# One first norm over seven tiles: the memory's tokens ahead of the rows, with the memory's key and value projection woven in

## The chip, the cores and the metric

The kernel runs on one core of a Trainium2 chip. The metric is the device time of one execution in microseconds. Engines are named as in the profile: PE is TensorE (PEld its weight loads), DVE is VectorE, ACT is ScalarE, POOL is GpSimd, SP is SyncE, which here issues nearly all DMAs. All data is float32. A large product is made in three matmuls on float32r operands: each operand is split into a high part (ACT casts it) and a low part (DVE or POOL subtracts the high part from the original), and high x high, low x high and high x low are summed in PSUM.

## The reference

Two transformer blocks run one after the other. The parts that the change touches, shortened:

```python
h = concatenate([meta, x])                       # 16 + 512 tokens, 1024 wide
u = rmsnorm(h, mix_norm_g);  proj = u @ w_in     # block 1: token mixer, then
h = h + token_mixer(u)                           # an expert-choice FFN with
h = h + expert_choice_ffn(rmsnorm(h, ffn_norm_g))#   16 experts
...
mkv = rms_norm(mem, mem_norm_w) @ w_mem_kv       # block 2: mem is 256 x 1024,
mk, mv = split(mkv)                              #   w_mem_kv 1024 x 1536
mqn = rms_norm(mq, mem_q_norm_w); mk = rms_norm(mk, mem_k_norm_w)
y_mem = softmax(mqn @ mk.T * 192**-0.5) @ mv     # 4 heads of 192
merged = g0*(y_ssd @ w_ssd_br) + g1*(y_dil @ w_dil_br) + g2*(y_mem @ w_mem_br)
h = h + merged @ w_out
h = h + peer(rms_norm(h, norm_ffn_w))            # 16384 experts, top 16 x 8
```

`mem` is an input: its norm and its product with `w_mem_kv` depend on nothing that either block computes.

## The kernel before, in words

The program is a sequence of blocks (`nc.Block()`); in each, every engine has its own list of instructions, and all engines meet at the block's end. Beside the block's own work runs a **feed** (class `Feed`): a list of weight chunks (1024 x 256 columns, 1 MB) and of jobs on them. A job is one PSUM result (128 tokens x 256, or 128 channels x 264 or 512), made in 24 matmuls when k is 8. The feed is cut into **ticks**, one job each, and every block is allotted some ticks; each engine's list holds its part of a tick at a place written out by hand:

- SP (L602): loads the next chunk into one of two raw slots, after the low part of the chunk in that slot was taken (`low_done`); also stores results that go to DRAM.
- ACT (L691): casts a chunk's high part, after the last job on the chunk two before it (`product_done`).
- POOL (L711): subtracts to get the low part. For the very first chunk DVE does it (`first_low`, L702).
- PE (L630 to L652): job n, after the result of job n - `banks` was taken out of PSUM (`taken`). `banks` is 2 in block 1's mixer (`proj_mix`) and 3 in block 2's merge (`proj_br`).
- `take_out`: in tick t the engine named by a job (ACT or DVE) takes out the job of tick t - (banks - 1), in its program order.

`normalise` (L134 to L330) does a norm with transposition: for tile n of 128 rows ACT squares and sums (L179), DVE forms 1/(mean + eps), ACT takes the root (L214) and scales (L187), PE transposes in 8 matmuls (L317), DVE multiplies by the gain (L254), ACT takes the high part two tiles later (`take_high`, L193) and DVE the low part (`take_low`, L258). In block 1's first norm (`norm1`, five tiles: four of x and the 16 meta tokens) the feed has one tick, in which the first chunk is split; the jobs begin in the next block.

In block 2 the merge (L3590 to L3660) runs these blocks, each with ticks of `proj_br`: `load_mem` (mem and two gains; 3 ticks), `norm_mem` (the memory's norm; 5), `turn_ssd` (4), `norm_mq` (`rms_groups` over the four query tiles; 6), `turn_mq` (2), a bare `run_to` (2, and x comes back from DRAM), `norm_mk` (2), `turn_mk` (1), and `attend` (L2464), the attention to the memory in 18 rounds, with 3 ticks, at rounds 5, 11 and 17. The jobs are 8 for the dilated branch (k = 2, DVE takes them out), 12 for the memory's keys and values (`mkv_jobs`, ACT takes them out into `mkv`), 8 for the SSD branch (DVE: a product with the gate and a sum), then 8 for the memory branch and 16 for `w_out`.

`norm2`, ahead of the experts' routing, loads `gain_row` at its own beginning (L293), and DVE waits for it before anything else.

Of the kernel before, what the change touches and what calls it, by code (L numbers as in the profile page):

```python
# [23 lines left out]
P = 128  # L24
# [109 lines left out]
def normalise(nc, name, x, tiles, gain_col, ident, xT, gain_row=None, kept=None, feed=None, prime=False, loads=(), late_loads=(),  # L134
              ahead=None, tile_product=None, tile_loads=None, side_loads=()):

    n_tiles = len(tiles)
    split = isinstance(xT, tuple)  # L140
    with Stage(nc, name) as st:
# [12 lines left out]

        def turned_of(n):
            return turned[:, n % 2, :].rearrange("p (k c) -> p k c", k=KD)[:, :, 0:tiles[n][1]]
# [4 lines left out]
        def part(buf, n):  # L161
            _, rows, col = tiles[n]
            return buf[:, :, col:col + rows]

# [4 lines left out]
        with nc.Block() as block:  # L169

            @block.scalar
            def _(act):
                def square(n):
# [5 lines left out]
                    act.activation(squares[:rows, :] if kept is None else kept[:rows, i, :], x[:rows, i, :],  # L179
                                   ACT.Square, accum_out=ssq[:rows, n:n + 1]).then_inc(squared, 1)  # L180

                def scale_here(n):
# [4 lines left out]
                    act.activation(row(n), x[:rows, i, :], ACT.Copy, scale=rstd[:rows, n:n + 1]  # L187
                                   ).then_inc(scale_done, 1)

                def take_high(n):  # L190
                    if kept is None:
                        act.wait_ge(gain_done, n + 1)
                        act.copy(part(xT[0], n), to_split(n)).then_inc(high_done, 1)  # L193
                    elif split:
                        act.wait_ge(turn_done, n + 1)
                        act.copy(part(xT[0], n), to_split(n)).then_inc(high_done, 1)
                    else:
                        act.wait_ge(turn_done, n + 1)
                        act.copy(part(xT, n), turned_of(n)).then_inc(evac_done, 1)
                    if feed is not None and not prime:  # L200
                        feed.act(act, n + 1, n_tiles + 1)
# [5 lines left out]
                for n in range(n_tiles):  # L207
# [11 lines left out]
                    if prime and n == n_tiles - 2:  # L219
                        feed.act(act)  # L220
                for n in range(max(0, n_tiles - 2), n_tiles):
                    take_high(n)

            @block.vector
            def _(dve):
                order = InOrder(dve, dve_order)
                dve.memset(ssq[:, :], 1.0).then_inc(cleared, 1)
                if loads:
                    dve.wait_ge(loaded, 16 * len(loads))
                if feed is not None:  # L230
                    feed.dve(dve, 0, n_tiles + 1)
# [8 lines left out]
                def scale(n):  # L240
                    i, rows, _ = tiles[n]
                    dve.wait_ge(rooted, n + 2)
# [3 lines left out]
                def apply_gain(n):  # L246
# [6 lines left out]
                    gain = gain_col.unsqueeze(2).broadcast_to([P, KD, rows])  # L253
                    dve.tensor_tensor(to_split(n), turned_of(n), gain, ALU.mult).then_inc(gain_done, 1)  # L254

                def take_low(n):
                    dve.wait_ge(high_done, n + 1)
                    dve.tensor_tensor(part(xT[1], n), to_split(n), part(xT[0], n).bitcast(F32),  # L258
                                      ALU.subtract).then_inc(evac_done, 1)
                    if feed is not None:  # L260
                        feed.dve(dve, n + 1, n_tiles + 1)

                behind = 2 if kept is not None else 1 if feed is None or prime else 0
                invert(0)
                for n in range(n_tiles):
# [8 lines left out]
                if prime:  # L274
# [3496 lines left out]
```

## Time and profile before

| what | us |
|---|---|
| median of 3 runs | 4327.09 (4322.07 to 4329.12) |
| the profiled execution | 4337.45 |
| its span | 4335.6 |
| PE busy | 4023.7 (93%) |
| DVE busy | 3022.6 (70%) |
| ACT busy | 2296.2 (53%) |
| POOL busy | 1200.4 (28%) |
| granted TensorE clock, mean | 0.961 of full |
| first block (norm1) | 0 to 27.1 |
| norm2 | 487.5 to 507.5 |
| merge, `load_mem` to the end of `attend` | 2719.5 to 2919.5 |

The profiled execution took 1.85 us more than its span, and 10.4 us more than the median of the runs. A busy share of PE is not its share of peak: a matmul at half clock, and one whose end is modelled, counts as busy as well. [...]

### The profile page before, as it was taken

How to read it: one execution, taken by the hardware profiler on the slowest of the kernel's cores; microseconds unless marked ns; L12 is line 12 of the kernel's file. 1: busy time of each engine (PE TensorE's matmuls, PEld its weight loads, DVE VectorE, ACT ScalarE, POOL GpSimd, SP SyncE). 2: the span in 40 equal slices, each digit the busy share in tenths (PEclk: the TensorE clock that was granted, in tenths of full speed). 3: DMA queues.
4: the chain of work that ended last, by engine and by line, in shares of the span. 5: the costliest groups of instructions: out<-in, count | busy, mean ns of one | idle time of the engine just before them, and what ended most of it. 6: DMA issues, size and time to landing. Idle time of an engine off the chain costs nothing. (4 is left out here: it accounts for less than half of the span.)

```text
span 4335.6 us, 58000 instructions
## 1 busy us (share of the span) xinstructions
PE 4023.7 (93%) x21773; PEld 3180.7 (73%) x21773; DVE 3022.6 (70%) x3734; ACT 2296.2 (53%) x2943; POOL 1200.4 (28%) x555
## 2 busy tenths in 40 slices
PE   8888599999999999999699899788999999999999
PEld 7776566666666666666589777667889999978887
DVE  4365478888888888888445532443599777788885
ACT  4432266777776767776344345322237988333332
POOL 2210201000000100000222221312254555666762
PEclk9999799999999999999899899788999999999999
DMA  3211479999999999998323331413256999999995
GB/s 101 90 63 61 154 306 370 368 372 373 370 363 369 380 368 374 374 378 326 129 90 114 136 99 40 141 58 99 84 194 212 327 349 346 364 350 368 367 368 190
DMA packets 294884, 1082.18 MB, mean 250 GB/s; under 512 B 23234, under 2 KB 163778, under 8 KB 246568
## 3 DMA queue, kind: packets, MB, share of 16 engines
q1 hardware_dynamic: 254136, 936.49, 57.9%
q0 software_dynamic: 40560, 143.16, 8.9%
q8 instruction: 121, 1.98, 0.2%
q14 instruction: 67, 0.55, 0.0%
HBM read 1001.57 MB, written 77.97 MB: 249 GB/s over the span
## 5 line engine op out<-in xcount | busy, mean ns | idle before, releaser
L1789 ACT CAST moe_expert_high<-moe_expert_raw 128x2048 fp32r<-128x2048 f32 x570 | 973.4, 1759 | 383.2 <-DMA moe_expert_raw<-in_w_down_blocks 121.2
L1558 DVE TENSOR_TENSOR moe_expert_low<-moe_expert_raw,moe_expert_high 128x2048 fp32r<-128x2048 f32 x380 | 817.5, 2197 | 170.7 <-ACT moe_expert_high L1789 170.2
L3124 ACT CAST peer_high<-peerbuf_table_raw 128x1024 fp32r<-128x1024 f32 x256 | 256.0, 1049 | 432.9 <-PE peer_ps L3107 281.0
L711 POOL TENSOR_TENSOR branches_proj_low<-branches_proj_raw,branches_proj_high 128x2048 fp32r<-128x2048 f32 (+3 forms) x58 | 246.5, 4250 | 683.7 <-ACT branches_proj_high L691 627.8
L1676 POOL DMA_INDIRECT scratch_h<-ffn_result,ffn_y_rows x16 | 65.2, 4074 | 1223.0 <-DVE ffn_result L1828 1223.0
L1558 DVE TENSOR_TENSOR ffn_expert_low<-moe_expert_raw,moe_expert_high 128x2048 fp32r<-128x2048 f32 (+1 forms) x192 | 362.6, 1929 | 52.2 <-ACT moe_expert_high L1789 52.1
L3078 PE MATMUL peer_ps<-peerbuf_hnT_high,peer_high 128*128 128x384 f32 x1024 | 352.6, 344 | 5.2 <-ACT peer_high L3124 5.2
L3079 PE MATMUL peer_ps<-peerbuf_hnT_low,peer_high 128*128 128x384 f32 x1024 | 345.1, 337 | 0.0
L2927 DVE TENSOR_TENSOR peer_low<-peerbuf_table_raw,peer_high 128x1024 fp32r<-128x1024 f32 x185 | 255.7, 1410 | 123.4 <-ACT peer_high L3124 121.9
L1718 PE MATMUL ffn_gate_p<-moe_expert_high,ffn_x_high 128*66 128x512 f32 (+1 forms) x768 | 284.1, 376 | 1.2 <-DVE ffn_x_low L1858 1.2
L1719 PE MATMUL ffn_gate_p<-moe_expert_high,ffn_x_low 128*66 128x512 f32 (+1 forms) x768 | 283.1, 375 | 0.0
L1718 PE MATMUL ffn_up_p<-moe_expert_high,ffn_x_high 128*66 128x512 f32 (+1 forms) x768 | 282.5, 374 | 0.0
L1719 PE MATMUL ffn_up_p<-moe_expert_high,ffn_x_low 128*66 128x512 f32 (+1 forms) x768 | 282.3, 374 | 0.0
L1745 PE MATMUL ffn_down_p<-moe_expert_high,ffn_t_high 128*66 128x512 f32 x704 | 280.0, 398 | 0.3 <-ACT moe_expert_high L1789 0.3
L1747 PE MATMUL ffn_down_p<-moe_expert_high,ffn_t_low 128*66 128x512 f32 x704 | 277.2, 394 | 0.0
L2927 POOL TENSOR_TENSOR peer_low<-peerbuf_table_raw,peer_high 128x1024 fp32r<-128x1024 f32 x71 | 185.7, 2620 | 231.4 <-ACT peer_high L3124 231.4
L3107 PE MATMUL peer_ps<-peer_high,peerbuf_hnT_high 128*128 128x512 f32 x768 | 238.6, 392 | 9.9 <-DVE peerbuf_hnT_low L3194 6.1
L3107 PE MATMUL peer_ps<-peer_low,peerbuf_hnT_high 128*128 128x512 f32 x768 | 237.4, 390 | 0.0
L3107 PE MATMUL peer_ps<-peer_high,peerbuf_hnT_low 128*128 128x512 f32 x768 | 237.4, 390 | 0.0
L3088 PE MATMUL peer_ps<-peerbuf_hnT_high,peer_low 128*128 128x384 f32 x1024 | 202.1, 339 | 6.8 <-DVE peer_low L2927 5.9
L3078 PEld LDWEIGHTS peer_ps<-peerbuf_hnT_high,peer_high 128*128 128x128 f32 x1024 | 194.6, 190 | 5.4 <-ACT peer_high L3124 5.4
L711 POOL TENSOR_TENSOR mix_proj_mix_low<-mix_proj_mix_raw,mix_proj_mix_high 128x2048 fp32r<-128x2048 f32 (+2 forms) x24 | 90.0, 3749 | 386.0 <-ACT mix_proj_mix_high L691 386.0
(552 smaller groups left out, 9425.3 us busy)
## 6 DMA issues: line engine op xcount, KB each, us to landing
moe_expert_raw<-in_w_gate_blocks SPq DMA_DIRECT2D x80, 2048.0 KB, 9.2
moe_expert_raw<-in_w_up_blocks SPq DMA_DIRECT2D x80, 2048.0 KB, 9.5
moe_expert_raw<-in_w_down_blocks SPq DMA_DIRECT2D x80, 2048.0 KB, 9.9
peerbuf_table_raw<-in_peer_down_t SPq DMA_DIRECT2D x64, 1024.0 KB
peerbuf_table_raw<-in_peer_up_t SPq DMA_DIRECT2D x64, 1024.0 KB
branches_proj_raw<-in_w_in SPq DMA_DIRECT2D x36, 1024.0 KB, 5.3
scratch_a<-peer_gelu SPq DMA_DIRECT2D x64, 384.0 KB
scratch_g<-peer_spread SPq DMA_DIRECT2D x24, 1024.0 KB
```

The lines of the kernel that those rows point to most:

```text
L711: pool.tensor_tensor(owner.slot_of(owner.low, at), owner.slot_of(owner.raw, at), owner.slot_of(owner.high, at).bitcast(F32), ALU.subtract) ...
L1558: return engine.tensor_tensor(self.half_of(self.low, q, h), self.half_of(self.raw, q, h), self.half_of(self.high, q, h).bitcast(F32), ALU. ...
L1718: pe.matmul(out, x_high[:, k, 0:CAP], hi[:, k, :], start=(k == 0), stop=False)
L1719: pe.matmul(out, x_low[:, k, 0:CAP], hi[:, k, :], start=False, stop=False)
L1745: pe.matmul(down_p[:CAP, cols], t_high[:, s, t, 0:CAP], hi[:, t, cols], start=(c == 0 and t == 0), stop=False)
L1747: pe.matmul(down_p[:CAP, cols], t_low[:, s, t, 0:CAP], hi[:, t, cols], start=False, stop=False)
L1789: act.copy(half_of(high, q, h), half_of(raw, q, h)).then_inc(high_done, 1)
L2927: return engine.tensor_tensor(low[:, q % 2, cols], raw[:, q % PR_RAW, cols], high[:, q % 2, cols].bitcast(F32), ALU.subtract)
L3078: pe.matmul(out_t, d_high[:, j, k, :], hn_high[:, k, 0:DTOK], start=(k == 0), stop=False)
L3079: pe.matmul(out_t, d_high[:, j, k, :], hn_low[:, k, 0:DTOK], start=False, stop=False)
L3107: last = pe.matmul(ps[:, 2 * t + half, :], lhs, right[:, q % 2, cols], start=(b == 0 and j == 0 and c == 0 and right is high), stop=(b == ...
L3124: act.copy(high[:, q % 2, cols], raw[:, q % PR_RAW, cols]).then_inc(high_done, 1)
```

## The change

- `normalise` can take a `head`: tiles of another buffer, with a gain and a result of their own, that pass ahead of its tiles; and a list `beside` that puts feed ticks behind each tile on ACT, DVE and PE. `norm1` now passes seven tiles: two of `mem`, four of x, the meta tokens. The 12 key and value jobs are the first of `proj_mix`; DVE takes them into staging, and SP stores them to a new DRAM buffer `mkv_dram`. `beside=[[], [0], [], [1, 2, 3], [4, 5, 6], [7, 8], [9, 10], [11, 12]]`.
- In SP's list the loads are mem 0, mem 1, identity, two column tables, x 0, x 1, then tick 0 of the feed, then x 2, x 3, the meta tokens, then the other ticks.
- In the merge `norm_mem`, the 12 jobs, the bare `run_to` and `norm_mk` are gone. `load_mem` loads `mkv` from DRAM. `turn_ssd` has 3 ticks. `norm_mq` and `norm_mk` are one `rms_groups` over six tiles (`norm_mqk`, 7 ticks), and x comes back there. `turn_mq` has 1 tick, `turn_mk` 1, `attend` 1, at round 17.
- `gain_row` of `norm2` is loaded during the last stretch of the mixer; DVE waits for it only before it scales the first tile. The router's weights are issued ahead of the feed's part.

The core of the diff:

```diff
@@ normalise, ACT
+                    ticks_at(feed.act if beside else None, act, n)
                 for n in range(max(0, n_tiles - 2), n_tiles):
                     take_high(n)
+                ticks_at(feed.act if beside else None, act, n_tiles)
@@ normalise, DVE
                         apply_gain(n)
+                    if beside and n == 1:
+                        feed.first_low(dve)
                     if split and n >= behind:
                         take_low(n - behind)
+                    ticks_at(feed.dve if beside else None, dve, n)
...
+                ticks_at(feed.dve if beside else None, dve, n_tiles)
@@ normalise, SP
                         for to, at in side_loads:
                             sp.dma_start(to, at).then_inc(side_in, 16)
+                    if n == 3 and beside:
+                        feed.sp(sp, 0, beside[-1][-1] + 1)
@@ normalise, PE
                     last.then_inc(turn_done, 1)
+                    if beside and beside[n] and n == n_mem + 1:
+                        pe.wait_ge(evac_done, n_mem)
+                    ticks_at(feed.pe if beside else None, pe, n)
@@ first_block
+            def memory(n):
+                return [Job("token", 0, 256, lambda nc, ps, slot: nc.vector.tensor_copy(slot, ps), "dve", col=col, rows=rows,
+                            store=mkv_dram[i, :, n * 256:(n + 1) * 256]) for i, rows, col in mem_tiles]
...
+                      head=(mem, cols_2[:, a:a + n], mem_uT, N_MEM // P),
+                      beside=[[], [0], [], [1, 2, 3], [4, 5, 6], [7, 8], [9, 10], [11, 12]])
...
-                          loads=[(gain_row[:, :], io["ffn_g_row"].partition_broadcast(P))],
+                          gain_in=gain_in,
@@ second_block
-                feed.allot_to(dil_end)
-                normalise(nc, "norm_mem", mem, mem_tiles, gain("mem_g"), ident, mem_uT, feed=feed)
-                feed.allot(4)
+                feed.load("load_mem", [(mkv[:, i, :], mkv_dram[i]) for i in range(N_MEM // P)] +
...
+                feed.allot(3)
                 turn_rows(nc, "turn_ssd", y_ssd, SEQ_TILES, ident, ssdS, feed=feed)
-                feed.allot(6)
-                rms_groups(nc, "norm_mq", [mq[:, i, :] for i in range(NT)], HEADS, MEM_HD, q_gain[:, :], feed)
+                feed.allot(7)
+                rms_groups(nc, "norm_mqk", [mq[:, i, :] for i in range(NT)] + [mkv[:, i, 0:MEM_W] for i in range(N_MEM // P)],
+                           HEADS, MEM_HD, [q_gain[:, :]] * NT + [k_gain[:, :]] * (N_MEM // P), feed,
+                           [(x[:, 0:NT, :], x_dram, x_back)])
-                feed.allot(2)
+                feed.allot(1)
                 turn_rows(nc, "turn_mq", mq, SEQ_TILES, ident, mqT, MEM_W // P, feed)
-                feed.run_to(mkv_end + feed.lag, lambda sp: sp.dma_start(x[:, 0:NT, :], x_dram).then_inc(x_back, 16))
-                mem_side.stack.close()
-                feed.allot(2)
-                rms_groups(nc, "norm_mk", [mkv[:, i, 0:MEM_W] for i in range(N_MEM // P)], HEADS, MEM_HD,
-                           k_gain[:, :], feed)
```

## Rows read from the trace of the kernel before

**Rows 1.** The page, 40 slices of the span: granted clock in tenths.

```profile
PEclk9999799999999999999899899788999999999999
```

**Rows 2.** Timeline of the first block: start, duration (us), engine, line, operation.

```profile
2.61 0.91 SPq L288 DMA_DIRECT2D top_h<-in_x  x2
...
17.57 1.88 ACT L691 CAST mix_proj_mix_high<-mix_proj_mix_raw 128x2048 fp32r<-128x2048 f32 x1
...
17.72 1.97 PE L317 MATMUL norm_turned<-top_ident,norm_scaled 128*128 128x128 f32 x8 [1.58 <-ACT norm_scaled L187]
...
22.88 1.22 DVE L258 TENSOR_TENSOR mix_uT_low<-norm_gained,mix_uT_high 128x1024 fp32r<-128x1024 f32 x1
...
24.01 2.28 DVE L702 TENSOR_TENSOR mix_proj_mix_low<-mix_proj_mix_raw,mix_proj_mix_high 128x2048 fp32r<-128x2048 f32 x1
...
27.14 0.56 PE L642 MATMUL mix_proj_mix_out<-mix_uT_high,mix_proj_mix_high 128*128 128x264 f32 x1 [4.50 <-PEq L169]
...
32.23 0.28 PE L642 MATMUL mix_proj_mix_out<-mix_uT_high,mix_proj_mix_high 128*128 128x264 f32 x1
...
35.14 0.28 PE L642 MATMUL mix_proj_mix_out<-mix_uT_high,mix_proj_mix_high 128*128 128x264 f32 x1
```

**Rows 3.** Windows (busy time by engine, clock, DMA share, GB/s): first block's last transfers.

```profile
14.00:15.00 1.00, 0.82 (x4) 0.83 (x5) 1.00 (x1) 1.00 (x3) 0.00 (x0) 1.00 0.72 227
```

**Rows 4.** Windows of the merge's blocks, same columns; `turn_mk` (8.0 us) left out.

```profile
2719.50:2730.90 11.40, 6.77 (x18) 5.07 (x18) 0.69 (x1) 1.26 (x3) 2.53 (x2) 0.76 0.84 285
2730.90:2756.40 25.50, 13.87 (x46) 9.87 (x46) 8.67 (x14) 10.66 (x14) 6.32 (x2) 0.72 0.33 109
2756.40:2777.00 20.60, 17.88 (x128) 17.71 (x128) 6.09 (x6) 8.23 (x9) 9.16 (x2) 0.85 0.45 154
2777.00:2804.20 27.20, 18.00 (x144) 17.43 (x144) 24.49 (x14) 10.68 (x14) 14.45 (x3) 0.92 0.52 172
2804.20:2815.80 11.60, 11.30 (x72) 11.13 (x72) 3.74 (x4) 2.44 (x3) 4.56 (x1) 0.74 0.28 90
2815.80:2827.40 11.60, 11.14 (x48) 8.93 (x48) 0.00 (x0) 2.45 (x3) 4.60 (x1) 1.00 0.78 272
2827.40:2848.40 21.00, 13.28 (x48) 10.23 (x49) 12.91 (x12) 3.59 (x4) 4.50 (x1) 0.84 0.12 38
...
2856.40:2919.50 63.10, 60.40 (x232) 42.28 (x232) 28.18 (x86) 18.22 (x50) 3.49 (x1) 0.84 0.12 42
```

**Rows 5.** Timeline of `norm_mq`: POOL's splits and DVE's elementwise operations.

```profile
2782.68 9.88 POOL L711 TENSOR_TENSOR branches_proj_low<-branches_proj_raw,branches_proj_high 128x2048 fp32r<-128x2048 f32 x2 [7.15 <-ACT branches_proj_high L691]
...
2783.03 5.06 DVE L2137 TENSOR_TENSOR branches_mq<-branches_mq,norm_mq_ssq 128x768 f32<-128x768 f32 x1 [1.00 <-ACT norm_mq_ssq L2118]
...
2799.77 0.96 DVE L2137 TENSOR_TENSOR branches_mq<-branches_mq,norm_mq_ssq 128x768 f32<-128x768 f32 x1
```

**Rows 6.** `attend` on PE (timeline), and one window of it.

```profile
2869.32 2.21 PE L2489 MATMUL mem_scores<-merge_mkT,merge_mqT 128*128 128x256 f32 x4
...
2873.36 2.37 PE L2489 MATMUL mem_scores<-merge_mkT,merge_mqT 64*128 64x256 f32 x4
...
2876.98 0.88 PE L642 MATMUL merge_proj_br_out<-ssdside_ssdS_high,branches_proj_high 128*128 128x512 f32 x1
...
2883.32 1.22 PE L2489 MATMUL mem_scores<-merge_mkT,merge_mqT 128*128 128x256 f32 x4
...
2885.49 1.33 PE L2489 MATMUL mem_scores<-merge_mkT,merge_mqT 64*128 64x256 f32 x4
...
2872.00:2876.00 4.00, 4.00 (x12) 2.63 (x12) 1.39 (x5) 0.97 (x3) 0.00 (x0) 0.50 0.01 2
```

**Rows 7.** `norm2`, timeline: ACT's first square, and what DVE waited for.

```profile
487.95 1.06 ACT L179 ACTIVATE routebuf_u<-top_h 128x1024 f32<-128x1024 f32 x1
...
492.04 0.15 DVE L237 TENSOR_SCALAR norm_ssq<-norm_ssq 128x1 f32<-128x1 f32 x1 [4.37 <-DMA routebuf_gain_row<-in_ffn_g_row]
...
492.72 1.28 DVE L243 SCALAR_TENSOR_TENSOR routebuf_u<-top_h,norm_rstd,routebuf_gain_row 128x1024 f32<-128x1024 f32 x1
```

More of the change, by code:

```diff
@@ L134, in normalise @@
 def normalise(nc, name, x, tiles, gain_col, ident, xT, gain_row=None, kept=None, feed=None, prime=False, loads=(), late_loads=(),
-              ahead=None, tile_product=None, tile_loads=None, side_loads=()):
+              ahead=None, tile_product=None, gain_in=None, tile_loads=None, side_loads=(), head=None, beside=()):
+    mem, mem_gain, mem_T, n_mem = head or (None, None, None, 0)
+    tiles = [(i, P, P * i) for i in range(n_mem)] + list(tiles)
     n_tiles = len(tiles)
@@ L159, in to_split, with part, taken @@
             return gained[:, n % 2, :, 0:tiles[n][1]] if kept is None else turned_of(n)
-        def part(buf, n):
+        def part(half, n):
             _, rows, col = tiles[n]
+            buf = mem_T[half] if n < n_mem else xT[half] if split else xT
             return buf[:, :, col:col + rows]
+        def taken(n):
+            i, rows, _ = tiles[n]
+            return mem[:rows, i, :] if n < n_mem else x[:rows, i, :]
         def row(n):
@@ L227, in _ @@
                 dve.memset(ssq[:, :], 1.0).then_inc(cleared, 1)
-                if loads:
-                    dve.wait_ge(loaded, 16 * len(loads))
-                if feed is not None:
+                if feed is not None and not beside:
                     feed.dve(dve, 0, n_tiles + 1)
@@ L241, in scale @@
                     i, rows, _ = tiles[n]
+                    if n == 0 and loads:
+                        dve.wait_ge(loaded, 16 * len(loads))
+                    if n == 0 and gain_in is not None:
+                        dve.wait_ge(gain_in, 16)
                     dve.wait_ge(rooted, n + 2)
@@ L257, in take_low @@
                     dve.wait_ge(high_done, n + 1)
-                    dve.tensor_tensor(part(xT[1], n), to_split(n), part(xT[0], n).bitcast(F32),
+                    dve.tensor_tensor(part(1, n), to_split(n), part(0, n).bitcast(F32),
                                       ALU.subtract).then_inc(evac_done, 1)
-                    if feed is not None:
+                    if feed is not None and not beside:
                         feed.dve(dve, n + 1, n_tiles + 1)
-                behind = 2 if kept is not None else 1 if feed is None or prime else 0
+                behind = 2 if kept is not None else 1 if feed is None or prime or beside else 0
                 invert(0)
@@ L306, in _ @@
             def _(pe):
-                if feed is not None:
+                if feed is not None and not beside:
                     feed.pe(pe, 0, n_tiles + 1)
@@ L319, in _ @@
                     last.then_inc(turn_done, 1)
-                    if feed is not None:
+                    if beside and beside[n] and n == n_mem + 1:
+                        pe.wait_ge(evac_done, n_mem)
+                    ticks_at(feed.pe if beside else None, pe, n)
+                    if feed is not None and not beside:
                         feed.pe(pe, n + 1, n_tiles + 1)
@@ L327, in _ @@
                             tile_product(pe, n - 1)
+                ticks_at(feed.pe if beside else None, pe, n_tiles)
                 if tile_product is not None:
@@ L2091, with rms_groups @@
 COLS_2_N = sum(c for _, c in COLS_2.values())
-def rms_groups(nc, name, xs, groups, width, gain, feed=None):
+def rms_groups(nc, name, xs, groups, width, gain, feed=None, loads=()):
     n = len(xs)
@@ L2156, in _ @@
                 def _(sp):
+                    for dst, src, landed in loads:
+                        sp.dma_start(dst, src).then_inc(landed, 16)
                     feed.sp(sp)
```

83 lines of the change are left out of this document (48 added, 35 removed).

## The prediction

> **What bounds the kernel now.** The page first: TensorE is busy for 93% of the span and its granted clock is near full in most slices [rows 1]. So the span is a row of stages that mostly end on TensorE, and because all engines meet at each block's end, what one block gains or loses goes straight into the total. I therefore read the two places that change, one window per block, and ask in each what ends last. The first block (0 to 27.1) has no jobs: its pace is ACT's, which squares, takes the root, takes a high part and scales for each tile, and makes room for the first chunk's cast at 17.57 [rows 2]. In the merge, eight windows [rows 4] show that few blocks are full of TensorE work: `norm_mem` holds 13.9 us of it in 25.5, `norm_mk` 13.3 in 21.0. `norm_mq` is DVE's (24.5 of 27.2). There the reader must see one thing: an elementwise DVE operation takes 0.96 us by itself and 5.06 beside a POOL split [rows 5]. It starts at 2783.03, the first of two splits runs from 2782.68 for 4.94, and DVE ends when that split has. It waits and then runs; it isn't slower work. `attend` has two paces. Its score matmuls start 4.04 us apart (2869.32, 2873.36) and, after the feed's job at 2876.98, 2.17 apart (2883.32, 2885.49) [rows 6]. [...]
>
> **The first block, step by step.** Bytes ahead of the second weight chunk's end are what they were, 4 MB: they ended in the window 14 to 15 [rows 3], so the first chunk lands near 11.9, a chunk being 1 MB at some 350 GB/s. ACT casts it after scaling mem tile 1: 11.9 to 13.8 (1.88 [rows 2]). DVE's `first_low` then takes 2.28, to 16.3. SP has meanwhile reached tick 0, which also holds the load of chunk 2, and that waits for this low part. **Behind it in SP's queue stand x 2, x 3 and the meta tokens**, which before were issued from 2.61 on, ahead of any weight [rows 2]. They are issued at 16.7 and x 2 lands near 22.5 to 23 (1.5 MB ahead of it, plus 2 us). ACT squares x 2 before it takes mem tile 1's high part and scales x 1: that ends at 26.5, transposes (1.97 [rows 2]) at 28.5, and the jobs may begin.
>
> A 24-matmul job takes 5.1 us at the low rate and 2.9 at the high one: starts at 27.14, 32.23, 35.14 [rows 2]. (The clock column says 1.00 there; the distance of the starts says otherwise.) Jobs 0 and 1 end at 36.2. Job 2 needs bank 0, which DVE empties in a tick that stands behind `take_low` of x 0. That needs ACT's `take_high`, which stands behind ACT's cast of chunk 2, which needs job 1. So each round is a closed circle: job, cast 1.9, square and root 1.3 (while tiles are left), high 1.0, low 1.2, take-out 0.4, next job. Beside `take_low` runs POOL's split of the chunk just cast, 4.6 us. Both inputs of `take_low` lie in SBUF, as those of the 5.06 us row do, so I let it end 1.1 after POOL's end. The trace has no `take_low` beside a split; its bounds are 1.22 [rows 2] and about 4.6 + 1.1. I take the second, since the nearest row is of the same operation. Then: take-out 44.4; job 2, transposes, job 3 to 53.4; cast 55.6, POOL to 60.4, low 61.5; jobs 4 and 5, transposes, job 6 to 73.8, with the cast of chunk 4 from 70.2, POOL to 76.9, low 78.0; job 7 from 78.4, the meta transposes and job 8; cast of chunk 5 to 85.1, POOL to 89.9, low 91.0; jobs 9, 10, 11 to 102, the low part of the first conv chunk at 103.1. TensorE rests 5 to 8 us in each circle, so I give each first job the low rate. The next block starts at 103.8, not 27.1: **+76.7**. Without any wait of `take_low` the four circles shorten by 2.4, 2.4, 3.4 and 3.7: +64.8. The next block's first job then runs warm: **-2.4** (5.1 to 2.9, rounded up). Stores and SP's later waits end ahead of their casts and cost nothing: chunk 3's load waits for a low part at 32.5 and its cast comes at 53.7. If they slipped by one circle it would cost up to 5.
>
> [...]
>
> **The merge, block by block** (before [rows 4], then after). `load_mem`: 11.4, +1.3, as 1.5 MB come where 1 MB did. `norm_mem`: -25.5. `turn_ssd`: 20.6; its four jobs of 24 matmuls become three of six, 15.6 if TensorE is at the low clock; -5.0. `norm_mqk`: six squares and reductions to 7.0, two take-outs to 8.4, then 12 elementwise operations where there were eight. Two of them stand behind the splits of chunks 4 and 5 (to 17.8), ten take 1.0: 27.8. Now the wait that the change adds: the jobs here are the SSD branch's, and **DVE takes them out**, where ACT took the memory's. With three banks TensorE can do job 8 alone and then stands until DVE has done all 12. Jobs 9 to 12 follow: 7.8 (cold start), then 5.5 each, to 52.9; POOL's last split ends at 54.1. 54.8 in all: against 27.2, +27.6. `turn_mq`: one job for two, -1.1. `run_to` -11.6 and `norm_mk` -21.0 are gone, `turn_mk` is alike. `attend`: two jobs fewer, but the remaining one comes at round 17. Up to round 5 all is as before, low clock included: 20.6 us, from 2856.4 to the job at 2876.98 [rows 6]. Then ten more rounds at 4.04 (bounds 2.17 and 4.04; I take the second, for the reason above), two short ones without scores, estimated at 4.7, the job 6.3 (2876.98 to 2883.32), the end 0.8: 72.8 against 63.1, +9.7. Sum of the merge: 1.3 - 25.5 - 5.0 + 27.6 - 1.1 - 11.6 - 21.0 + 9.7 = **-25.6**.
>
> `norm2`: DVE stood for 4.37 until the gain had landed [rows 7]; the first square runs from 487.95 for 1.06, so with DVE's two small operations and the root the first scaling can start at 489.8, not 492.72 [rows 7]: **-2.9** (0 if the experts' loads set the end there). The router's load, one place earlier in SP's queue, is not waited for.
>
> **Sum:** 76.7 - 2.4 - 25.6 - 2.9 = +45.8. Against the profiled execution, 4337.45, that is 4383.3. That execution is 10.4 above the median of the runs, so for a median: 4327.1 + 45.8 = **4373**.
>
> **The rivals.**
> **B, the attention runs at the full clock.** If it is not at 0.50 from its third round on, or comes back without a job, 16 rounds take 2.17, the two short ones 3.7, a warm job 5.6 and the end 0.8: 44.8 instead of 72.8, so 28.0 less, 4345. Against it: the window at 0.50 with 4.00 busy, and nothing dense before round 17 [rows 6]. For it: the block's mean is 0.84 [rows 4], so most of its rounds ran at 1.00 and stayed there between jobs; a slight shift at its start could keep the clock up.
> [...]
> **C, faster: TensorE sets the pace.** The hand-offs of the first block hide behind jobs, TensorE never rests long enough to lose its clock, and the block ends near 70: from 28.5, 12 jobs at 2.9, three transposes of 1.0 or less, 2.2 for the cold start and the last split. Then +42.9 - 2.4 - 2.9 and, with B's attention, -53.6: -16.0, 4311. It decides from a point that can be named: with `attend` at full clock the rest saves 53.6 + 2.9 + 2.4 = 58.9, so the kernel is faster if the first block ends before 27.1 + 58.9 = 86. Against it: the circle above is in the program's order and can't be passed.
> **D, the loads are not sooner.** Were x 2 not held behind chunk 2, the block would be 6 us shorter: 4367. Were it held longer (chunk 2's megabyte and the split both late), 5 us more: 4378. Both lie in my own range.
>
> **How the numbers follow.** Forecast with D 0.66: 4355 to 4388, the lower end without the wait of `take_low` (-12) and some 5 of slack in `norm_mqk`, the upper with slipped stores, a POOL split more in `norm_mqk` (+4.3) and cold jobs throughout. B 0.22: 4330 to 4356. C 0.08. The rest lies between B and C. A difference of 0.2%, 8.7 us, is about what a measurement of this kernel can tell from none. Faster takes C, 0.08; the same the lower edge of B and the rest, 0.10; slower 0.82. The range reaches from B's lower end, 4330, to 4390.
>
> **What would show it.** Right: the first conv job near 104; PE idle 5 to 8 us before jobs 2, 4, 7 and 9; `take_low` of 3 to 5 us beside POOL; x 2's square at 22 or later; in `norm_mqk` a TensorE gap of some 10 us and four jobs after it; `attend` at 0.50 for over 50 us. Wrong: a first block that ends before 90, or `attend` at 1.00. The first would mean that the circle is shorter than its rows, the second that the clock depends on more than the job.

## The result, and the profile after

The changed kernel takes 4360.86 us (median of 6 runs, 4351.27 to 4369.17) beside 4326.52 for the kernel before: ratio 1.0073, 95% interval 1.0055 to 1.0092, some 34 us slower. A second set of runs gave 1.0066 (1.0048 to 1.0085), 30 us. The profiled execution is 4364.41, its span 4362.6; before it was 4337.45 and 4335.6, so the two traces differ by 27.0.

The first cut lays the same landmarks of both traces side by side (us from the span's start, each the first start of an instruction that both kernels have). I took the profile of each kernel a second time, unedited, to see what scatters by itself:

| landmark | before | before, again | after | after, again |
|---|---|---|---|---|
| block behind the first norm | 27.2 | 27.6 | 104.1 | 104.4 |
| `norm2`, first square | 487.9 | 488.8 | 564.2 | 561.3 |
| experts, first product | 546.8 | 546.7 | 621.2 | 618.2 |
| `fin_gains` (behind the experts) | 2074.1 | 2076.3 | 2154.4 | 2146.2 |
| `turn_dil` | 2714.8 | 2717.0 | 2798.5 | 2788.8 |
| attention (`mem_scores`) begins | 2856.4 | 2856.0 | 2901.5 | 2891.7 |
| `turn_mem` (attention ended) | 2919.7 | 2910.3 | 2954.4 | 2944.5 |
| `outS` products begin | 2964.2 | 2953.3 | 2997.4 | 2987.5 |
| peer stage's first index | 3145.9 | 3135.0 | 3172.5 | 3162.7 |

In the first pair (before, after) the first block costs 76.9, `turn_dil` to `outS` gives 50.5 back, and the stretch behind it gives 6.6 that I had not forecast. The experts' stage, which no edit touches, is 5.9 longer; over the twelve profiles of changed and edited kernels it took 1521.6 to 1541.4 us, so this is its own scatter, and a difference of a few us has to be read block by block, not from a total.

**The first block after.** ACT, POOL, DVE and PE on the timeline (start, duration, engine, line, operation, in brackets the idle time ahead and what ended it):

```profile
22.94 1.06 ACT L190 ACTIVATE norm_squares<-top_h 128x1024 f32<-128x1024 f32 x1 [5.56 <-DMA top_h<-in_x]
...
35.48 1.90 ACT L718 CAST mix_proj_mix_high<-mix_proj_mix_raw 128x2048 fp32r<-128x2048 f32 x1 [7.52 <-PE mix_proj_mix_out L675]
...
37.45 4.51 POOL L738 TENSOR_TENSOR mix_proj_mix_low<-mix_proj_mix_raw,mix_proj_mix_high 128x2048 fp32r<-128x2048 f32 x1 [4.81 <-ACT mix_proj_mix_high L718]
...
39.48 3.56 DVE L273 TENSOR_TENSOR normed_uT_low<-norm_gained,normed_uT_high 128x1024 fp32r<-128x1024 f32 x1 [10.03 <-ACT normed_uT_high L204]
42.97 0.74 DVE L2004 COPY mix_proj_mix_staging<-mix_proj_mix_out 128x256 f32<-128x256 f32 x2
43.43 0.58 PE L665 MATMUL mix_proj_mix_out<-mix_proj_mix_high,memside_mem_uT_high 128*128 128x256 f32 x1 [8.05 <-DVE mix_proj_mix_staging L2004]
...
60.54 0.58 PE L665 MATMUL mix_proj_mix_out<-mix_proj_mix_high,memside_mem_uT_high 128*128 128x256 f32 x1 [8.04 <-DVE mix_proj_mix_staging L2004]
76.82 0.58 PE L665 MATMUL mix_proj_mix_out<-mix_proj_mix_high,memside_mem_uT_high 128*128 128x256 f32 x1 [4.35 <-DVE mix_proj_mix_staging L2004]
90.41 0.58 PE L665 MATMUL mix_proj_mix_out<-mix_proj_mix_high,memside_mem_uT_high 128*128 128x256 f32 x1 [4.31 <-DVE mix_proj_mix_staging L2004]
...
85.28 4.73 DVE L273 TENSOR_TENSOR normed_uT_low<-norm_gained,normed_uT_high 128x1024 fp32r<-128x1024 f32 x1 [1.92 <-ACT normed_uT_high L204]
...
104.11 0.06 DVE L2051 MEMSET conv_padded<- 128x4 f32 x1 [4.68 <-PEq L180]
```

The reader is to see one turn of the circle in the rows from 35.48 to 43.43: cast, POOL's split beside `take_low`, take-out, next job. It comes four times. `take_low`, 1.22 alone [rows 2], takes 3.56, 3.55, 4.63 and 4.73.

**The merge after**, one window per block: `load_mem`, `turn_ssd`, `norm_mqk`, `turn_mq`, `turn_mk`, `attend`, and from there to `outS` (columns as in [rows 4]: busy time of PE, weight load, DVE, ACT, POOL, then clock, DMA share, GB/s):

```profile
2803.80:2816.20 12.40, 7.12 (x18) 5.35 (x19) 0.69 (x1) 1.24 (x2) 2.54 (x2) 0.64 0.88 300
2816.20:2828.60 12.40, 10.09 (x50) 8.52 (x50) 6.68 (x7) 4.60 (x6) 1.29 (x1) 0.84 0.48 154
2828.60:2883.70 55.10, 34.61 (x132) 27.37 (x133) 31.46 (x30) 13.95 (x12) 18.32 (x4) 0.81 0.38 136
2883.70:2894.20 10.50, 9.95 (x48) 8.27 (x48) 5.03 (x6) 0.00 (x0) 0.00 (x0) 0.84 0.35 121
2894.20:2901.50 7.30, 6.98 (x36) 5.69 (x36) 4.72 (x4) 1.48 (x2) 3.51 (x1) 1.00 0.13 34
2901.50:2954.40 52.90, 50.00 (x184) 33.67 (x185) 25.64 (x82) 16.85 (x49) 0.00 (x0) 0.81 0.06 21
2954.40:2997.40 43.00, 36.16 (x168) 29.49 (x169) 27.24 (x32) 15.02 (x17) 15.39 (x4) 1.00 0.38 129
```

In `norm_mqk` TensorE is busy for 34.6 of 55.1. Its timeline shows the two elementwise operations that stand beside splits, and the wait behind all 12:

```profile
2835.88 4.56 POOL L738 TENSOR_TENSOR branches_proj_low<-branches_proj_raw,branches_proj_high 128x2048 fp32r<-128x2048 f32 x1 [10.68 <-ACT branches_proj_high L718]
...
2837.37 3.89 DVE L2187 TENSOR_TENSOR branches_mq<-branches_mq,norm_mqk_ssq 128x768 f32<-128x768 f32 x1 [0.68 <-ACT norm_mqk_ssq L2168]
...
2841.29 5.27 DVE L2192 TENSOR_TENSOR branches_mq<-branches_mq,merge_q_gain 128x768 f32<-128x768 f32 x1
...
2857.26 0.80 PE L669 MATMUL merge_proj_br_out<-ssdside_ssdS_high,branches_proj_high 128*128 128x512 f32 x1 [11.94 <-DVE merge_merged L3449]
```

**The attention after** is where the forecast missed most. Two windows of it:

```profile
2905.00:2921.00 16.00, 15.87 (x42) 10.35 (x41) 6.50 (x21) 4.31 (x14) 0.00 (x0) 0.51 0.00 0
2921.00:2944.00 23.00, 22.16 (x102) 14.76 (x100) 15.42 (x52) 10.14 (x32) 0.00 (x0) 0.97 0.00 1
```

The clock is at its lower level for some 17 us (a window 2905.40:2922.50 has 0.50, with TensorE busy for 17.10 of 17.10 us) and then at the higher one, and no dense job is near: the block's only one starts at 2946.99. I had let ten more rounds run at the low level.

**The stretch behind the merge.** The peer stage's norm goes through the same function as the two that I had looked at. Before, the load of its keys stood in SP's queue behind the load of a third weight chunk, which waits for a low part, and the block then waited for it to land. Two timeline rows of before, and from the table of waits of SP in that window what it waited for (total, times, longest):

```profile
3029.98 0.58 SPq L297 DMA_DIRECT2D query_keys<-in_sub_keys  x1
...
3037.85 0.77 PE L642 MATMUL query_proj_query_out<-peerbuf_hnT_high,query_proj_query_high 128*128 128x512 f32 x1 [8.42 <-PEq L169]
```

```profile
SPq L303 <- DMA query_keys<-in_sub_keys: 6.8, 1, 6.8
```

After, the same rows; the wait is not in the table any more:

```profile
3048.05 2.85 SPq L318 DMA_DIRECT2D query_keys<-in_sub_keys  x1
...
3064.18 0.77 PE L669 MATMUL query_proj_query_out<-peerbuf_hnT_high,query_proj_query_high 128*128 128x512 f32 x1 [2.70 <-PEq L180]
```

8.42 falls to 2.70, and this norm's first transpose waits 6.80 where it waited 8.08, since DVE no longer waits for the gain ahead of its small operations. In both executions of before the stretch from `outS` to the first index is 181.7, in all changed kernels 174.7 to 175.7. No run moves these loads alone, so the share of each is read from the timeline.

### The profile page after: what moved, and what is told of

It reads as the page before. It is cut to its first block and busy times, and to the rows that moved or that the text cites. A ratio compares the mean times of both kernels' runs of the same rounds, so it can differ in the third digit from the quotient of the medians.

```text
span 4362.6 us, 57998 instructions
## 1 busy us (share of the span) xinstructions
PE 4032.5 (92%) x21773; PEld 3187.1 (73%) x21773; DVE 3029.0 (69%) x3743; ACT 2292.4 (53%) x2929; POOL 1186.0 (27%) x555
## 5 line engine op out<-in xcount | busy, mean ns | idle before, releaser
L738 POOL TENSOR_TENSOR branches_proj_low<-branches_proj_raw,branches_proj_high 128x2048 fp32r<-128x2048 f32 (+3 forms) x52 | 218.1, 4194 | 665.5 <-ACT branches_proj_high L718 615.0
L738 POOL TENSOR_TENSOR mix_proj_mix_low<-mix_proj_mix_raw,mix_proj_mix_high 128x2048 fp32r<-128x2048 f32 (+2 forms) x30 | 118.4, 3947 | 433.8 <-ACT mix_proj_mix_high L718 433.8
```

The source lines that it names most:

```text
L738: pool.tensor_tensor(owner.slot_of(owner.low, at), owner.slot_of(owner.raw, at), owner.slot_of(owner.high, at).bitcast(F32), ALU.subtract) ...
```

## The experiments

Every kernel below is compared with the kernel before on the same chip. Seven edits were made to the changed kernel one at a time; three combinations and two repeats followed. Code is that of the changed kernel.

**1. The held load.** SP issues x 2, x 3 and the meta tokens ahead of the load that waits.

```
+                    if n == 3 and beside:
+                        feed.first_loads(sp)
-                    if n == 3 and beside:
+                    if n == n_tiles - 1 and beside:
                         feed.sp(sp, 0, beside[-1][-1] + 1)
```

> Edit: x 2, x 3 and the meta tokens are issued in SP's queue right behind the first two weight chunks, ahead of the load of chunk 2 that waits for a low part. Theory of the held load (as predicted): the changed kernel's ACT stands 5.56 us before the square of x 2 at 22.94; without the hold x 2 has landed near 17, the first job starts near 22.3 instead of 27.84, and all that follows moves with it: the first block ends near 98.6 instead of 104.1, 4355.4 instead of 4360.9. Rival, the start of the jobs hangs on something else (POOL's split of chunk 1, or TensorE's order): the square moves and the block's end doesn't, 4361.

Measured: 4353.11, ratio 1.0063 (1.0044 to 1.0083). The time alone can't tell this from the changed kernel; the timeline can:

```profile
17.05 1.04 ACT L190 ACTIVATE norm_squares<-top_h 128x1024 f32<-128x1024 f32 x1
```

x 2's square moves from 22.94 to 17.05, the block's end from 104.11 to 96.25: 5.9 from the load, 1.0 in the first job (3.5 us where it took 4.5, since its matmuls go from 0.41 to 0.28 us each after 1.0 us of the job and not after 3.4) and 0.9 in the two circles behind it. Rival D's price is right, and by where it starts the held load is a cause.

**2. The take-out ahead of the low part.**

```
-                    if split and n >= behind:
-                        take_low(n - behind)
                     ticks_at(feed.dve if beside else None, dve, n)
+                    if split and n >= behind:
+                        take_low(n - behind)
```

> Edit: in the first norm DVE takes out the jobs' results of a tile ahead of the low part of the tile before, not behind it. Theory of the circle (job, cast, high, low beside POOL, take-out, next job): the next job no longer waits for it, TensorE's gaps of 8.05, 8.04 and 4.35 us go or shrink below 3, and 12 jobs are paced by the two chunk slots, some 6 to 7 us for two jobs: from 27.84 an end of the first block near 75 (71 to 82) instead of 104.1, 4332 (4328 to 4339). Rival, ACT's own queue (cast, square, root, high, scale) is the pace: only the take-outs' place is gained, four times take_low and take-out less what ACT already covers, an end near 92 to 97, 4349 to 4354.

Measured: 4323.92, ratio 0.9997 (0.9982 to 1.0012): all of the loss is gone, by two lines exchanged; the time is below the expected 4328 to 4339, the block's end inside its range. The timeline:

```profile
38.49 3.58 DVE L273 TENSOR_TENSOR normed_uT_low<-norm_gained,normed_uT_high 128x1024 fp32r<-128x1024 f32 x1 [3.64 <-ACT normed_uT_high L204]
...
71.60 0.58 PE L665 MATMUL mix_proj_mix_out<-mix_proj_mix_high,memside_mem_uT_high 128*128 128x256 f32 x1 [4.50 <-DVE mix_proj_mix_staging L2004]
...
77.39 0.06 DVE L2051 MEMSET conv_padded<- 128x4 f32 x1 [5.52 <-PEq L180]
```

`take_low` is as slow as it was beside POOL (3.58), but where TensorE waited four times for a take-out behind it, it now does so once, for 4.50 ahead of the last job: the block ends at 77.39, 26.7 sooner. The circle is the cause of these 26.7; the rival, ACT's queue, had 92 to 97. The attention of this execution took 43.4 where the changed kernel's took 52.9, which would be the rest of the 37 us between the two medians; whether the edit brings that is open (below).

**3. POOL writes and reads nothing.** If it is POOL's split that `take_low` waits for, it falls from 3.56, 3.55, 4.63 and 4.73 us to 1.2 each beside an operation that reads nothing. Standing in the circle, that is 11.6 us out of the first block, whose end would come near 92.5, and 4349. If `take_low` is slow by its own operands or by ACT, or is not in the circle, the time stays at 4361.

```
+                    if 1 <= c < self.zero_low:
+                        pool.memset(owner.slot_of(owner.low, at).bitcast(F32), 0.0).then_inc(owner.low_done, 1)
+                        continue
```

> Leaves out the low part of the memory's weight chunks 1 to 5: POOL writes zeros there in place of its subtraction, so it reads nothing. [...]

Measured: 4337.82, ratio 1.0022 (1.0009 to 1.0035).

```profile
65.39 1.81 POOL L739 MEMSET mix_proj_mix_low<- 128x2048 f32 x1 [12.65 <-ACT mix_proj_mix_high L718]
...
66.41 1.23 DVE L273 TENSOR_TENSOR normed_uT_low<-norm_gained,normed_uT_high 128x1024 fp32r<-128x1024 f32 x1 [0.93 <-ACT normed_uT_high L204]
...
68.02 0.39 PE L665 MATMUL mix_proj_mix_out<-mix_proj_mix_high,memside_mem_uT_high 128*128 128x256 f32 x1 [0.94 <-DVE mix_proj_mix_staging L2007]
...
87.07 0.06 DVE L2055 MEMSET conv_padded<- 128x4 f32 x1 [4.85 <-PEq L180]
```

Beside a POOL operation that reads nothing `take_low` takes 1.23: the 11.6 us were the wait for POOL's split. Two of the four `take_low` (66.41 and 74.13) begin while POOL still writes, the other two 0.25 us after it has ended, since its writing takes 1.8 us where the split took 4.6. So only two places show that an operation which doesn't read leaves `take_low` alone. The block ends 17.0 sooner, not 11.6. The other 5.4 go with the clock: the two shorter waits fell from 4.35 and 4.31 to 0.94 and 0.93, and behind so short a rest the first matmul takes 0.39 where it took 0.58 (76.82). By the rows the jobs behind those two waits take 3.06 and 2.97 where they took 5.42 and 5.29. A shorter wait gave more than its length.

**4. The attention's job early.**

```
-                    feed.pe(pe, u, rounds)
+                    feed.pe(pe, *at(u))
```

The same for DVE and ACT; at(u) is (min(u, 2), 3) in the memory attention, and (u, rounds) elsewhere.

> Edit: the one job of the SSD branch in the memory attention comes behind round 2, not round 17. In the changed kernel the clock was at 0.50 from about 2905 to 2921 (16 us) and then at 1.00 with no job near. Theory J, as predicted, a dense job brings the clock back: it is at 1.00 within the job, some 6 to 8 us after the attention's start, most of the low rounds go, attention 46 to 48 us instead of 52.9, 4354 to 4356. Theory T, the clock comes back after a time of full busy whatever the work is: the low phase keeps its 16 us, the job lies in it and takes 10 us instead of 7, attention 51 to 53 us, 4359 to 4361.

Measured: 4346.67, ratio 1.0043 (1.0027 to 1.0059), the attention 47.6. The first matmuls of the job:

```profile
2901.68 0.88 PE L669 MATMUL merge_proj_br_out<-ssdside_ssdS_high,branches_proj_high 128*128 128x512 f32 x1
...
2904.06 0.63 PE L670 MATMUL merge_proj_br_out<-ssdside_ssdS_low,branches_proj_high 128*128 128x512 f32 x1
2904.49 0.53 PE L669 MATMUL merge_proj_br_out<-ssdside_ssdS_high,branches_proj_high 128*128 128x512 f32 x1
2904.86 0.40 PE L670 MATMUL merge_proj_br_out<-ssdside_ssdS_low,branches_proj_high 128*128 128x512 f32 x1
```

The full rate comes back inside the job, from 0.63 to 0.40 us a matmul at 2904.5, with the low stretch begun by 2897.9 (a score matmul of 2.34 there), so after some 7 us; in the changed kernel, without the job, it was 17. The time, 4346.67, is under what either theory expected. Before this is laid to the job, experiment 5 has to be seen, whose attention has its job at round 17 as the changed kernel's. Its low stretch, and that of this run:

```profile
2891.10:2901.30 10.20, 10.05 (x26) 6.26 (x25) 4.01 (x13) 3.33 (x11) 0.00 (x0) 0.50 0.03 10
2898.00:2904.80 6.80, 6.80 (x17) 4.93 (x18) 3.37 (x9) 1.74 (x6) 0.00 (x0) 0.50 0.00 0
```

So the stretch differs without a job too (10.2 and 17.1). With the job behind round 2 it was 6.8 in each of the three executions in which the clock fell, shorter than in any without, and that is all that can be said for the job.

**5. Take-outs between the elementwise operations of `norm_mqk`.**

```
                     order(dve.tensor_tensor(x, x, g, ALU.mult))
+                    if name == "norm_mqk":
+                        feed.dve(dve, 2 + i, 2 + n)
```

> Edit to the changed kernel: in norm_mqk DVE takes out the products a tile at a time between its 12 elementwise operations, where it took out all that were left behind the last. Theory (as predicted): TensorE's wait of 11.94 us in that block is for those take-outs, and goes: the block falls from 55.1 us to TensorE's seven jobs, 41 to 43, and the kernel with it by 10 to 13 (plus or minus the 9 us by which the attention behind it can catch either pace of the clock). Rival, DVE itself is the bound (6 reductions, 12 elementwise, 7 take-outs are 36 us by their rows, with POOL's splits over 40): the gap moves to the end, the block stays over 50.

Measured: 4346.10, ratio 1.0041 (1.0028 to 1.0054); the block 50.3, not 41 to 43. The rival came nearer, for a reason that neither had:

```profile
2834.06 5.20 DVE L2192 TENSOR_TENSOR branches_mq<-branches_mq,merge_q_gain 128x768 f32<-128x768 f32 x1
2839.30 0.69 DVE L3451 TENSOR_TENSOR merge_merged<-merge_proj_br_side,merge_proj_br_out 128x512 f32<-128x512 f32 x1
...
2840.04 0.80 PE L669 MATMUL merge_proj_br_out<-ssdside_ssdS_high,branches_proj_high 128*128 128x512 f32 x1 [8.16 <-DVE merge_merged L3451]
```

The first pair of operations lies beside two splits (3.85 and 5.20), and the first take-out lies behind the pair. A third split, later in the block, caught one more (5.25).

**6. Products first.** So the next form takes four products out ahead of the 12 operations (`feed.dve(dve, 4, 8)`, then one more behind every second tile), with the edits 1, 2 and 4.

> The four-edit form, but in norm_mqk DVE takes out four products ahead of its 12 elementwise operations and the last three behind the second, fourth and sixth tile. In the interleaved form TensorE still stood 8.16 us because two elementwise operations lay ahead of a take-out and waited for POOL's splits (3.85 and 5.20 us). If that wait is the cause: no gap over 3 us, seven jobs at about 5.1, the block 44 to 46 instead of 50.3, 4305 to 4309 where the four-edit form had 4311. Rival: DVE's work is only pushed to the block's end (12 operations, one beside a split), 50 or more, no gain.

Measured: 4303.14, ratio **0.9935 (0.9917 to 0.9953)**, 25 us faster than the kernel before. The block's window:

```profile
2794.50:2835.90 41.40, 32.69 (x132) 26.26 (x133) 32.18 (x30) 13.95 (x12) 19.23 (x4) 0.92 0.51 182
```

41.4 us with no wait of TensorE left inside the row of jobs but the 5.77 ahead of the first take-out. It is 13.7 less than in the changed kernel: the wait of 11.94, and some 2 us because the job behind that wait began at the low rate there (0.63 us a matmul up to 2860.8, then 0.39). It is less than I had expected because I had counted seven jobs at 5.1; two of the seven are the dilated branch's, of six matmuls each.

**7. Jobs in a block of their own.** The norm takes its seven tiles alone; `feed.run_to(end["mkv"])` behind it.

> Edit to the changed kernel: the first norm takes its seven tiles with no jobs beside; the 12 jobs of the memory's key and value run in a block of their own behind it. Theory of the circle: without tiles between, nothing but the two chunk slots paces the jobs. Norm to 33 to 34 (27.1 for five tiles and 3.1 for each more), one job cold at 5, eleven at 2.9, the low part of the next chunk: first block ends at 74 to 78 instead of 104.1, that is 4331 to 4335. It also tells whether work laid beside a norm is worth anything here: the takeout-first form had both at once and ended at 77.4. Rival, POOL's split of 4.6 beside casts of 1.9 is the pace and not the circle: 6.5 for each of six chunks and the cold start, an end near 84, 4341.

Measured: 4326.48, ratio 1.0002 (0.9992 to 1.0013), the first block ends at 74.24. Alone, the two parts take less than the 77.4 that the woven form takes in experiment 2. But this form frees the held loads as well, which experiment 2 does not; with both edits (experiment 8) the woven form ends at 71.6. So work beside the norm is worth 2.6 us at best. The time is again under the expected 4331 to 4335, with an attention of 43.4. What is late next is a store:

```profile
54.12 0.42 DVE L2004 COPY mix_proj_mix_staging<-mix_proj_mix_out 128x256 f32<-128x256 f32 x1 [3.83 <-DMA scratch_mkv<-mix_proj_mix_staging]
```

The four staging slots are full from there on; this wait comes three times (3.83, 3.90, 4.93). I had costed the stores at nothing; at the slower pace of the changed kernel they were.

**8. Combinations.** The edits 1, 2, 4 and 5:

> The changed kernel with four edits: x 2, x 3 and meta issued ahead of the held load, take-outs ahead of the low part in the first norm, take-outs between the elementwise operations of norm_mqk, the attention's one job behind round 2. If the places are independent, as the theory has it: first block 77.4 less 6 to 8 for the loads, end near 70; norm_mqk 12 less; attention 44 to 48. Against the kernel before: first block +43, merge 207.0 to about 140, norm2 -2.2: -22 to -26 in all, 4302 to 4306 beside 4328, ratio 0.995. Rival, the gaps are one and the same slack and fill each other (DVE or the clock takes back what one edit gives): 4318 or more.

Measured: 4311.37, ratio 0.9966 (0.9953 to 0.9978): first block 71.6, `norm_mqk` 50.3, attention 47.2. The places are independent, as each block is as long as with its own edit alone; the time lies between forecast and rival, and the sum fell short by what edit 5 did. And 7, 5 and 4 together:

> The changed kernel with the 12 memory jobs in a block of their own behind the norm, take-outs between the elementwise operations of norm_mqk, and the attention's one job behind round 2. By the theory: first block ends at 74 to 78, norm_mqk 12 less, attention 44 to 48: 4306 to 4312 beside 4328. Rival as for the other combination: 4322 or more.

Measured: 4318.44, ratio 0.9985 (0.9974 to 0.9996), with 74.6 and an attention of 46.8; its experts' stage was 1538.2, ten over most. It lies between forecast and rival, and the time doesn't decide.

**9. The attention with no job.** One more job to the block ahead (`feed.allot(2)` at `turn_mk`).

> Edit to the changed kernel: the attention's one job is given to the block ahead of it, so the attention has 16 rounds and no dense job at all. By the prediction's step (full busy time alone does not bring the clock back) it would stay at 0.50 to its end, 18 rounds near 4.04: 66 to 73 us for the attention. By the traces since (17 us low in two kernels, then 1.00 with no job near; no low phase in two others) it ends by itself after about 17 us, or isn't there: 46 us or 37 us, and the block ahead 5 to 6 us longer, so the kernel is where the changed one is, within 5 us.

Measured: 4346.97, ratio 1.0052 (1.0039 to 1.0065). The whole attention:

```profile
2897.70:2936.70 39.00, 35.14 (x161) 23.00 (x162) 23.98 (x80) 16.82 (x49) 0.00 (x0) 1.00 0.00 1
```

39.0 us at the full clock, with no dense job in it. By my step a fallen clock would have made it 66 or more; here it didn't fall, so this run doesn't show a return. The changed kernel's own two windows do. The edit also puts a second job directly ahead of the attention, which may have kept the clock up; no run tells.

**10. Both kernels again.**

> The changed kernel once more, unedited, for the spread of its runs (4351 to 4369) and for the blocks that no edit touches. If the attention's low phase is a matter of where its start falls, this execution shows it at 43 to 44 us or at 53, whichever; the experts' stage, 1527 to 1541 us in the profiles so far, again lies in that range. Nothing else moves: first block ends at 103 to 105, norm_mqk 55.

Measured: 4358.06, ratio 1.0066 (1.0048 to 1.0085); attention 52.8, experts 1528.0, first block 104.4.

> The kernel before once more, unedited. Its profiled execution was 10.4 us above the median of its runs, and the blocks behind the merge took 6.6 us less in every changed kernel (175 us from the last product's operands to the peer stage's first index, beside 181.7). If that is the one execution and not the change, this profile shows that stretch at 175 too, or the attention under 63.3, and its sum of blocks near 4327. If the change itself moved them: 181.7 and 63.3 again, and the surplus sits in the experts' stage (1527.3 before) or elsewhere.

Measured: 4329.70, ratio 1.0001 (0.9987 to 1.0014). `outS` to the first index is 181.7 again: that gain belongs to the change. The attention is not the same:

```profile
2856.00:2910.30 54.30, 51.40 (x232) 36.44 (x233) 27.81 (x86) 18.21 (x50) 3.49 (x1) 1.00 0.14 48
```

The kernel before, unedited, ran it once in 63.1 to 63.3 us with a low stretch [rows 4, 6] and once in 54.3 with none. All attentions that I have, each from its window (us, mean clock, and how long the stretch at 0.50 near its start lasted):

| job in the attention | executions |
|---|---|
| three, from round 5 on (before) | 63.3 at 0.84 (low for 20.5); 54.3 at 1.00 |
| one at round 17 (after and its forms) | 52.9, 52.8, 52.9 at 0.81 (low for 17.1 each); 47.7 at 0.89 (10.2); 43.5, 43.4, 43.4 at 1.00 |
| one behind round 2 | 47.6, 47.2, 46.8 at 0.93 (6.8 each); 44.8 at 0.98 (only its last 2 us) |
| none | 39.0 at 1.00 |

## Why the prediction was right and where it was wrong

**The first block was right, term by term.** Forecast end 103.8, measured 104.11 and 104.4. The take-outs that close the circles came at 42.97, 60.08, 76.36 and 89.94, where 44.0 (44.4 is its end), 61.5, 78.0 and 91.0 had been worked out: 1.0 to 1.6 sooner, and from one to the next 17.1, 16.3 and 13.6 where the forecast had 17.5, 16.5 and 13.0, so the circles themselves are right. Of TensorE's waits two (8.05, 8.04) were as said and two (4.35, 4.31) just under the 5 to 8 that I had named as the sign. Experiment 2 shows the circle, 3 the wait of `take_low` (11.6 by its rows, forecast 11.9; the time that it cost was 17.0), 1 the held load (5.9, forecast 6). The choice of the upper bound for `take_low` was right: the traces have 3.55 to 4.73 beside the split, and 1.22 to 1.23 in experiment 3, where POOL reads nothing.

**C** would have needed an end ahead of 86. It was at 104; experiments 2 and 7 reach 74 to 77 by changes of order, which is what C had assumed of the kernel as it stood. With the end there, and the attention at the full clock in the profiled execution, the kernel is level with before (0.9997, 1.0002) and not ahead, as C's point of 86 had it. C's saving counted on an attention of 63.1 before; the second profile shows 54.3.

**The next block's warm start** came: its first job takes 3.0 (first matmuls at 104.23 and 107.24) where it took 5.1. **`norm2`** gave 2.2 by its first scaling (564.24 to 566.81, before 4.77 [rows 7]) for 2.9.

**The merge** gave 49.6 up to the end of the attention, not 25.6:
- `norm_mqk` 55.1 (forecast 54.8), its wait 11.94 (forecast some 10), two contended operations, four jobs behind them: right. `turn_mq` 10.5, right.
- `turn_ssd` 12.4, not 15.6: the clock rose within it, from 0.64 in the block ahead to 0.84. I had it low throughout: 3.2.
- **`attend` 52.9, not 72.8: 19.9, the step that failed.** That full busy time alone doesn't bring the clock back, but a dense job does, I took from one window [rows 6], behind which the return fell together with a job. The ten rounds at 4.04 in my sum stand on it, and no run shows them. The whole of that stretch, of which I had looked at 4 us:

```profile
2858.00:2878.00 20.00, 19.54 (x48) 12.75 (x49) 8.00 (x26) 5.46 (x17) 0.00 (x0) 0.50 0.12 43
```

It had lasted 19 us when the job began at 2876.98, and ended 1.5 us later. A job isn't needed: in the changed kernel the clock came back after 17.1 us without one, in experiment 5 after 10.2, and in five executions it never fell (in a sixth only at the end). So my sign, 0.50 for over 50 us, failed, and of **B** the mechanism held (it comes back without a job, or doesn't fall), but not its price: 44.8 was met only in the executions in which the clock stayed up (43.4 to 43.5). It came back without denser work, after 17.10 of 17.10 us busy at 0.50, and what brings it back stays open. I should have asked the trace for the same situation elsewhere before I let ten rounds hang on one coincidence.

**What the prediction left out:** the peer stage's norm. The diff moves `late_loads` ahead of the feed's queue for all calls of `normalise`; I followed that for `norm2`, where nothing waits for it, and not for the call of the peer stage, where 6.8 us did. -6.6, twice measured. Every caller of a changed function has to be gone through.

**The sum.** 45.8 - 19.9 (attention) - 3.2 (`turn_ssd`) - 6.6 (peer norm) is 16.1, and with the small terms (next block and `norm2` 2.5 less gain, `turn_mk` and the rest of the merge 0.7 more) 17.9. The medians say 30 to 34. The difference is in the kernel before: its profiled execution had the low stretch in the attention, and 10.4 us over its median; the second, at 54.3, was 1.4 over its own. Against an attention of 54.3 before and 52.9 after, the change of that block is -1.4, 9.0 less gain, and the sum 27; the two second profiles differ by 27.7 up to the peer stage's first index. What remains, 3 to 7 us, may lie in the scatter of the experts' stage (20 us between executions) and in how often each kernel has the low stretch, which 14 profiles don't settle. So the forecast was 12 above the median, less than its errors of 19.9, 6.6 and 3.2 add up to, because it also took its own attention of before, 63.1, for what that kernel always does. That was luck: with the errors mended and the 63.1 kept, the sum would have said 4345, below the 4355 at which the main range begins.

**Open** is what sets whether the attention's clock falls. Experiments 1, 2 and 7 change nothing within 2400 us ahead of it, and it didn't fall there; experiment 3 doesn't either, and it fell, as it did in the changed kernel twice out of two. The clock had gone another way already in `norm_mqk`, whose second low stretch was 10.2 us in experiments 1, 2 and 7 and 13.6 in the changed kernel and experiment 3; but it was 13.6 in experiment 12 too, whose attention stayed at 1.00. Where the blocks' starts fall in time is a guess that was not tested by itself.

## What to carry to other kernels

When jobs are laid beside other work, write out the closed circle of hand-offs, one engine's list at a time, and see what stands ahead of the take-out in its engine's program order: here one exchange of two lines was worth 27 us, and work beside the norm, once it was laid well, 2.6 us. Put take-outs of another unit's product ahead of an engine's own elementwise work, above all ahead of what will stand beside a POOL split: here a DVE operation on 128x768 took 0.96 us alone and 3.89 and 5.27 beside two splits of 4.6 (`norm_mqk` of the changed kernel). And go through every caller of a changed helper: a load that waits in a queue can hold back a load behind it in a stage that the change doesn't name.

## What was not expected of the hardware

- A wait of TensorE can cost more than its length, by the clock behind it: four waits shortened by 11.5 us in all gave 17.0 back (experiment 3), with first matmuls of 0.39 behind a rest of 0.94 and of 0.58 behind one of 4.35.
- The same block of the same kernel took 63.3 and 54.3 us in two executions by the clock alone (mean 0.84 and 1.00): TensorE was busy for 60.4 and 51.4 us, so its waits were the same. The changed kernel's took 52.9 and 52.8, and 43.4 in edited kernels that leave that block as it is.
- A stretch at the low clock can last 17.1 us while TensorE is busy for all of it (changed kernel, 2905.40 to 2922.50), so a full busy share doesn't say that the clock is about to rise.
- Here a DVE operation that reads PSUM and SBUF wasn't held up inside a POOL split, and one with two SBUF inputs was. The split runs from 2866.83 for 4.60, to 2871.43; the first of the two operations has its 0.69, the second, 0.69 elsewhere, ends 0.54 after the split (`norm_mqk` of the changed kernel):

```profile
2866.83 4.60 POOL L738 TENSOR_TENSOR branches_proj_low<-branches_proj_raw,branches_proj_high 128x2048 fp32r<-128x2048 f32 x1 [21.08 <-ACT branches_proj_high L718]
...
2870.23 0.69 DVE L3451 TENSOR_TENSOR merge_proj_br_side<-merge_proj_br_side,merge_proj_br_out 128x512 f32<-128x512 f32 x1 [4.03 <-PE merge_proj_br_out L677]
2870.95 1.02 DVE L3453 TENSOR_TENSOR merge_merged<-merge_merged,merge_proj_br_side 128x512 f32<-128x512 f32 x1
```
